# Block two's mixer in a new order, its bias outside the matmuls, and norms by logarithm and exponential

## The reference

```
h = rmsnorm(x);  x = x + 0.5 * swiglu(h)
p = rmsnorm(x) @ w_in          # 2048 columns: a, f (256 each), q, k, v (512 each)
y_pool = ((window means of a) - a) @ pool_w * pool_scale      # 4 groups, windows 2, 4, 8, 16
y_four = real(fft2(f)) @ fourier_w                            # over tokens and 64 features
s_j = q_j k_j^T / 8 - slope_h * |i - k|     for 4 heads h and the two halves j of a head
attn = softmax(s_0) - lambda * softmax(s_1)
y_attn = rmsnorm(attn @ v) * head_norm * (1 - lambda_init)
x = x + concat(y_pool, y_four, y_attn) @ w_out
h = rmsnorm(x);  x = x + 0.5 * swiglu(h)
```

## Time and profile before

| | |
|---|---|
| median of 3 runs | 2199.71 us (2198.16 to 2203.26) |
| profiled execution | 2203.84 us, span 2202.0 us |
| mean granted TensorE clock | 0.971 |
| TensorE busy | 2092.7 us, 95% |
| VectorE, ScalarE busy | 64%, 44% |
| mixer and output projection of block two, layer one | 1373 to 1488 us |
| the same, layer two | 1881.5 to 1996.5 us |
| HBM | 155 GB/s over the span |

### The profile page before, as it was taken

How to read it: one execution, slowest core, us unless ns; L and a number is a source line. 1 busy time by engine, 2 the same in 40 slices (tenths; PEclk the granted TensorE clock), 3 DMA queues, 4 the chain that set the end, 5 groups by cost and what they waited for, 6 DMA issues and landing times.

```text
span 2202.0 us, 42635 instructions
## 1 busy us (share of the span) xinstructions
PE 2092.7 (95%) x16256; PEld 2013.1 (91%) x16256; DVE 1411.6 (64%) x2402; ACT 970.9 (44%) x1402; POOL 181.6 (8%) x215
## 2 busy tenths in 40 slices
PE   8999888999999998889997999989998999989997
PEld 8999776999999987789997999979998999969997
DVE  6764646876577555567746775467754775566765
ACT  4434554443443345444434444344444443444443
POOL 0001200400130030030003000000000000000000
PEclk9999989999999998899998999999999999999999
DMA  6553322445354532235544564425554555414553
GB/s 238 179 196 136 115 77 77 153 168 198 129 180 165 196 122 77 84 111 189 197 185 145 176 214 163 139 73 172 178 209 137 172 198 184 153 58 168 177 207 136
DMA packets 44368, 343.12 MB, mean 156 GB/s; under 512 B 4848, under 2 KB 5872, under 8 KB 6256
## 3 DMA queue, kind: packets, MB, share of 16 engines
q1 hardware_dynamic: 43536, 335.63, 44.0%
q0 software_dynamic: 736, 6.17, 0.8%
HBM read 340.73 MB, written 1.05 MB: 155 GB/s over the span
## 4 chain that ended last, share of the span: by engine, by line
PE 86%; DVE 7%; ACT 2%; issue 2%; DVEq 1%; DMA 1%; POOL 0%; ACTq 0%; POOLq 0%; SPq 0%
PE ps L505 27%; PE ps L506 26%; PE ps L507 26%; DVE w_lo L1486 1%; ACT w_hi L1037 1%; DVE x_lo L1542 1%; DVE rstd L1549 0%; PE ps L764 0%; DVE scratch L1942 0%; PE ps L878 0%; DMA raw<-in_w_up 0%; PE ps L755 0%; ACT x_hi L1092 0%; PE ps L909 0%; DVEq L1516 0%
## 5 line engine op out<-in xcount | busy, mean ns | idle before, releaser
L505 PE MATMUL ps<-x_hi,w_lo 128*128 128x256 f32 (+3 forms) x3648 | 1071.2, 294 | 55.0 <-DVE x_lo L1542 24.4
L506 PE MATMUL ps<-x_lo,w_hi 128*128 128x256 f32 (+3 forms) x3648 | 1058.9, 290 | 0.0
L507 PE MATMUL ps<-x_hi,w_hi 128*128 128x256 f32 (+3 forms) x3648 | 1056.7, 290 | 0.0
L1486 DVE TENSOR_TENSOR w_lo<-raw,w_hi 128x1024 fp32r<-128x1024 f32 (+1 forms) x588 | 752.8, 1317 | 136.5 <-ACT w_hi L1037 130.9
L505 PEld LDWEIGHTS ps<-x_hi,w_lo 128*128 128x128 f32 x3648 | 710.5, 195 | 72.9 <-issue 32.8
L1037 ACT ACTIVATE w_hi<-raw 128x1024 fp32r<-128x1024 f32 (+1 forms) x588 | 633.4, 1120 | 325.2 <-PE ps L507 313.9
L506 PEld LDWEIGHTS ps<-x_lo,w_hi 128*128 128x128 f32 x3648 | 710.4, 195 | 0.6
L507 PEld LDWEIGHTS ps<-x_hi,w_hi 128*128 128x128 f32 x3648 | 710.1, 195 | 0.0
L507 PE MATMUL ps<-hid_hi,w_hi 128*128 128x256 f32 (+1 forms) x1408 | 400.3, 284 | 0.0
L505 PE MATMUL ps<-hid_hi,w_lo 128*128 128x256 f32 (+1 forms) x1408 | 398.0, 283 | 0.0
L506 PE MATMUL ps<-hid_lo,w_hi 128*128 128x256 f32 (+1 forms) x1408 | 396.9, 282 | 0.0
(11 more groups left out here) (235 smaller groups left out, 1258.4 us busy)
## 6 DMA issues: line engine op xcount, KB each, us to landing
raw<-in_w_up SPq DMA_DIRECT2D x178, 1024.0 KB, 4.9
raw<-in_w_down SPq DMA_DIRECT2D x64, 1408.0 KB, 6.0
raw<-in_w_in SPq DMA_DIRECT2D x36, 1024.0 KB, 4.9
raw<-in_w_out SPq DMA_DIRECT2D x16, 1024.0 KB, 5.0
cst<-in_consts POOLq DMA_DIRECT2D x1, 2176.0 KB, 9.6
cst<-in_consts POOLq DMA_DIRECT2D x1, 1537.5 KB, 6.7
prm<-in_prm POOLq DMA_DIRECT2D x2, 690.0 KB, 8.2
h<-in_hidden SPq DMA_DIRECT2D x1, 1088.0 KB, 7.1
```

Source lines behind the costliest of these rows:

```text
L505: mm(dst, w_lo[:, j, cols], xa, start=first, stop=False)
L506: mm(dst, w_hi[:, j, cols], xb, start=False, stop=False)
L507: return mm(dst, w_hi[:, j, cols], xa, start=False, stop=last)
L1486: v.tensor_tensor(w_lo[:, j, c], raw[:, j, c], w_hi[:, j, c].bitcast(F32), ALU.subtract)\
```

## The change

1. Input units of block two in a new order, set by tables `F0, A0`, `Q`, `K`, `V`: f, f, then q and k of head 0, 1, 2, 3, then v0..v3, then a, a. The host permutes the columns. Three PSUM banks in turn instead of four.
2. The steps of the Fourier part and of the heads stand between the units. TensorE's queue is: units 0 to 4, transposes of f, 5, scores 0, 6, sums over tokens, 7, scores 1, 8, sums over features, 9, transposes 0, scores 2, 10, Fourier product, 11, scores 3, v0, 12, transposes 1, output 0, v1, 13, output 1, v2, 14, transposes 2, v3, mean squares of heads 0 and 1, 15, output 2, transposes 3. Transposes of a, output 3, mean squares of heads 2 and 3 with the window means, and the pool product stand before chunks 1, 2, 3 and 5 of the first pair of the output projection. VectorE's and ScalarE's queues are rewritten to match, with the weight splits one unit at a time.
3. A score group has no bias matmul: its matmuls for the two row halves stand next to each other. VectorE adds the bias (fp32, in `cst`, over constants of block one) while it takes the maximum, four tensor_tensor_reduce a head into `prob2`; the exponentials read `prob2`.
4. The result chunks get their own place, `cat_hi2` and `cat_lo2`, in the memory of the feed-forward's hidden state. The projection takes them in the order 2, 3, 4, 5, 6, 7, 0, 1.
5. Every norm: logarithm, drain, exponential of minus a half of it, on ScalarE straight into `rstd`. The reciprocals go, on the head outputs too. The table set for both is loaded where the one for the root was, and at the end of each output projection.
6. In block two's output projection the first six x chunks of the next feed-forward are formed before the last two residuals, the last two behind their own.
7. Block two's layers are written out on TensorE, ScalarE and VectorE. SyncE and GpSimd keep their loops.
8. The second load of constants leaves out the old tables and a third one brings the bias, 1 MB; GpSimd's bf16 copy goes.

```diff
 def att_s(hh):
-    bank = S2_BANK[hh]
-    if hh == 3:
-        pe.wait_ge(exp2_done.sem, exp2_done.at(l, 2))
+    pe.wait_ge(proj2_ready.sem, proj2_ready.at(l, K[hh] + 1))
+    if hh > 0:
+        pe.wait_ge(nm2_ready.sem, nm2_ready.at(l, 4 * hh))
     for i in range(2):
         for j in range(2):
-            dst = ps[:, bank + j, 256 * i:256 * i + T2]
-            mm(dst, pj[head_rows(j), 4 + hh, P * i:P * i + P], pj[head_rows(j), 8 + hh, 0:T2],
-               start=True, stop=False)
-            last = mm(dst, slope_bf[:, hh, :], absd_bf[:, i, :], start=False, stop=True)
+            last = mm(ps[:, S2_BANK + j, 256 * i:256 * i + T2], pj[head_rows(j), Q[hh], P * i:P * i + P],
+                      pj[head_rows(j), K[hh], 0:T2], start=True, stop=True)
     last.then_inc(s2_ready.sem, 1)
...
 def block(i):
-    if i >= 4:
-        pe.wait_ge(proj2_ready.sem, proj2_ready.at(l, i - 3))
-    narrow_unit(turn0 + i // 4, (i // 2) % 2, i % 2, ps[:, i % 4, 0:T2], T2)
+    if i >= IN_BANKS:
+        pe.wait_ge(proj2_ready.sem, proj2_ready.at(l, i - IN_BANKS + 1))
+    narrow_unit(turn0 + i // 4, (i // 2) % 2, i % 2, ps[:, i % IN_BANKS, 0:T2], T2)
...
 def maxima(hh):                                   # VectorE
+    dve.drain()
     dve.wait_ge(s2_ready.sem, s2_ready.at(l, hh + 1))
-    s, bank = hh % 2, S2_BANK[hh]
-    v.reduce_max(amax[:, s, :], ps[:, bank:bank + 2, :].rearrange("p j (i k) -> p (j i) k", i=2), AX_X)
-    dve.drain()
-    v.tensor_scalar(nmax[:, s, :], amax[:, s, :], -ATT_SCALE, None, ALU.mult).then_inc(nm2_ready.sem, 1)
+    s = hh % 2
+    for j in range(2):
+        for i in range(2):
+            c = 2 * j + i
+            v.tensor_tensor_reduce(out=prob2[:, s, c, :], in0=ps[:, S2_BANK + j, 256 * i:256 * i + T2],
+                                   in1=alibi[:, hh, i, :], scale=-ATT_SCALE, scalar=3.0e38,
+                                   op0=ALU.add, op1=ALU.min, accum_out=nmax[:, s, c:c + 1])\
+                .then_inc(nm2_ready.sem, 1)
...
 def root(number, T, eps):                         # ScalarE
     act.wait_ge(var_ready, number + 1)
-    fn(std[:, 0, 0:T], ps[:, 7, 0:T], ACT.Sqrt, bias=con(eps, 1)).then_inc(std_ready, 1)
+    fn(std[:, 0, 0:T], ps[:, 7, 0:T], ACT.Ln, bias=con(eps, 1))
+    act.drain()
+    fn(rstd[:, 0:T], std[:, 0, 0:T], ACT.Exp, scale=-0.5).then_inc(std_ready, 1)
...
-def root(number, T, layer_norm=False):            # VectorE
+def root(number):
     dve.wait_ge(std_ready, number + 1)
-    last = v.reciprocal(rstd[:, 0:T], std[:, 0, 0:T])
-    if layer_norm:
-        last.then_inc(rstd_ready, 1)
-    dve.drain()
...
 def out_proj(turn0, resid, rms, norm, T, gain=None):   # ScalarE
     for p in range(OUTB // 2):
         if p > 0:
             split_next(turn0 + p // 2, p % 2, W_NARROW)
-        if p == OUTB // 2 - 1:
+        last = p == OUTB // 2 - 1
+        if rms and last:
+            for k in range(2 * p):
+                high(P2, gain, k, T, T2)
+        if last:
             second_pair(turn0 + OUTB // 4, 0)
-            load_sqrt()
+            load_log_exp()
         if rms:
             for u in range(2):
                 square(norm, resid, 2 * p + u, T)
-    if rms:
-        for k in range(KD):
-            high(P2, gain, k, T, T2)
+                if last:
+                    high(P2, gain, 2 * p + u, T, T2)
...
+return {1: a_transposes, 2: last_output, 3: last_means, 5: pool_out}     # TensorE, end of mixer2
...
-with pe.Fori(0, DEPTH) as l:                      # and the same on ScalarE and VectorE
+for l in range(DEPTH):
```

More of the change, by code:

```diff
@@ L516, in narrow_unit, with first_pair @@
                 last.then_inc(unit_used, 1)
-            def first_pair(turn, event, bank, T, xs=None, before=None):
+            def first_pair(turn, event, bank, T, xs=None, before={}, order=range(KD)):
                 xa, xb = xs or x_of(T)
                 pe.wait_ge(lo_done, turn * 4 + 2)
-                for k in range(KD):
-                    if before and k == before[0]:
-                        before[1]()
-                    pe.wait_ge(x_ready, event * KD + (k + 1))
+                for n, k in enumerate(order):
+                    if n in before:
+                        before[n]()
+                    pe.wait_ge(x_ready, event * KD + (n + 1))
                     for u in range(2):
@@ L1584, in out_proj @@
                         split_next(turn0 + p // 2, p % 2, W_NARROW)
+                    last = p == OUTB // 2 - 1
+                    if gain and last:
+                        for k in range(2 * p):
+                            low(number, P2, gain, k, T, T2)
                     for u in range(2):
-                        if p == OUTB // 2 - 1 and u == 1:
+                        if last and u == 1:
                             lo_unit(turn0 + OUTB // 4, 1, 0, W_NARROW)
@@ L1589, in out_proj @@
                         resid(alpha, 2 * p + u, bank + u, T)
-                if gain:
-                    for k in range(KD):
-                        low(number, P2, gain, k, T, T2)
+                        if gain and last:
+                            low(number, P2, gain, 2 * p + u, T, T2)
             def layer_norm(norm, gain, bias, next_turn, T):
@@ L1972, in mixer2 @@
+                scale(2)
+                weights(5)
+                lambda_sum()
+                scale(3)
+                weights(6)
+                scale(4)
+                weights(7)
+                scale(5)
+                weights(8)
+                maxima(0)
+                scale(6)
+                weights(9)
+                sine_sums()
+                scale(7)
+                weights(10)
+                difference(0)
+                scale(8)
+                weights(11)
                 maxima(1)
-                difference(0)
@@ L2021, in _ @@
             dve.drain().then_inc(prm_free, 1)
-            root(3 * DEPTH, T2)
-            with dve.Fori(0, DEPTH) as l:
+            root(3 * DEPTH)
+            for l in range(DEPTH):
                 t0, q = l * TURNS2 + BLOCK2_TURN, l * 2 + 2 * DEPTH
```

556 lines of the change are left out of this document (319 added, 237 removed).

## The result

Measured: 2138.81 us (median of 4 runs, 2129.02 to 2145.04) against 2198.93 for the kernel before on the same chip, ratio 0.9722 with a 95% interval of 0.9678 to 0.9767: 60 us faster. Forecast were 2151 and a range from 2138 to 2171, as a ratio 0.978 to the median of 2199.71. So the median lies 0.8 us inside the lower edge of the range, and by the ratio (0.9722 x 2198.93 = 2137.8) the time is 0.2 us outside it; the gain was 60 us where the sum had 49.2. The miss is a size, and it has to be found among the terms.

What follows compares the result with a forecast made beforehand. TensorE, busy 95% of the span, was taken as the bound: its work, waits and lower clock. Savings of 30.0 (terms 1 to 3), 11.9 and 7.3 (terms 4 and 5) make 49.2 us: 2199.71 becomes 2151, range 2138 to 2171.

Steps and rivals of the forecast that it cites:

- terms 4 and 5: Block two's layers written out instead of looped, 11.9 us; thirteen norms by logarithm and exponential without the reciprocal, 7.3 us.
- terms 1 to 3: Block two's mixer with output projection: scores 8.2, waits 3.4, clock 3.4; together 15.0 us a layer, 30.0 for both.
- term 2: TensorE waits behind the mixer's last input block: 8.8 us a layer go, 5.4 new ones in the projection, 3.4 saved.
- The list of places: Projection waits: head one's low part 0.3, head three's 1.1, pool chunk 1.6, first residual 0.8, last feed-forward chunk 1.6 us.
- term 3: Low TensorE clock in block two's mixer: 4.4 us a layer to regain, 1.0 left unpaid, 3.4 counted.
- term 1: Block two's scores without bias matmuls, row halves paired: a head from 3.36 to 1.3 us, 8.2 us saved a layer.
- rival 5: More than forecast: the waits in the projection and all of the low clock go too, 2139 us; chance 0.06.
- the signs that the prediction named: Mixer: busy about 12 us less, groups 1.3, no input wait over 0.5, projection waits 1 to 1.6; turn gap under 3.

Runs made afterwards that it cites:

- w1: The changed kernel without the table load at the end of block two's output projection; 2138.11 us, ratio 0.9717 to the kernel before.
- w4: The changed kernel with four 512-column copies, each with a drain, ahead of each head's exponentials on ScalarE; 2143.00 us, ratio 0.9733 to the kernel before.
- w2: The changed kernel with three 512-column copies, each with a drain, ahead of the logarithm of the second pair's norms on ScalarE; 2142.42 us, ratio 0.9727.
- w3: The changed kernel with all eight input chunks of the next feed-forward made behind all eight residuals; 2144.05 us, ratio 0.9738 to the kernel before.
- m1: The kernel before with layers written out and new norms, minus block two's bias matmuls (bias left out of the result), old order of work; 2170.83 us, ratio 0.9861.
- b1: The changed kernel without the projection's table load, with 64 unused bytes per partition ahead of split x and 64 more ahead of split hidden units; 2118.62 us, ratio 0.9633.

## Why the prediction was off

The direction holds, terms 4 and 5 were right within 1 us, and the savings come from where terms 1 to 3 placed them. The failed step is the size of terms 1 to 3, 15.0 us a layer, where the stretch gives 20.0 (117.0 - 97.0), and above all the waits that term 2 left in the projection:

- **Waits (term 2), the main error.** Forecast 8.8 - 5.4 = 3.4, measured 8.7 - 2.5 = 6.2. The list of places was right, the sizes were not: 0.3, 1.1, 1.6, 0.8 and 1.6 became 0, 0.56, 0.55, 0.16 and 1.20. For the second of them the trace says how it came to be too large (TensorE in the changed kernel, up to the row of 1426.60 above):

```profile
1422.23 1.02 PE L989 MATMUL ps<-scratch,cst 128*128 128x256 f32 x4
1423.18 1.95 PE L924 MATMUL ps<-cst,scratch 128*64 128x256 f32 x16
1425.07 0.39 PE L507 MATMUL ps<-hid_hi,w_lo 128*128 128x256 f32 x1
```

The chain from the mean squares to the chunk takes 4.37 us (1422.23 to 1426.60), even a little more than the 4.2 of the prediction. But TensorE works 3.81 of them: 0.95 for the mean squares, which the chain holds too, 1.89 for the window means and 0.97 for the chunk, where I had set only 1.9 and 0.72 against it (and 4.2 less these two is 1.6, not the 1.1 that I wrote). So the cover was too small there, not the chain too long. For the table load w1 shows that of the 1.28 us charged 0.46 was paid. For the pool chunk and the first residual the prediction gives no working, and why they came out at a third and a fifth stays open. w4 shows how well the chains ahead of all this are covered: of 11.2 us of delay 1.8 came through.
- **Clock (term 3).** Forecast 3.4, with 1.0 left unpaid; all 4.4 came back. Even the 4.1 us of waits in w2 left it at 1.00. That the waits are why it fell before is argued, not shown: for it speak the place (2.46 us and four more waits in some 24 us) and layer one of w3, against it that layer two of w3, with the longer wait, kept the full clock.
- **Scores (term 1).** Forecast 8.2; a group went from 3.19 to 1.06, 8.5 (it was 3.27 where a transpose followed, which can add 0.2 here and take it from the remainder below). I took both ends a little high: 3.36 counted a fourth bias in full, and two times 0.66 counted the changing over twice. That the whole of it appears on the path needs the new order: m1 gets 4 to 5.
- **Own place of the result chunks,** counted at nothing: 192 matmuls now stream from the faster tile, 0.0021 us each, 0.4. With small work that I did not price, the remainder is 0.9.

Together 2.8 + 1.0 + 0.3 + 0.9 = 5.0 a layer, 10.0 for both, which with 49.2 makes 59, against 60 measured. That is the figure of rival 5 (the waits in the projection and all of the low clock go too, 2139), to which I had given 0.06 and at which I had closed the range. Its mechanism came true only in part: all of the low clock went, but 2.5 of the 5.4 us of waits stayed, and the scores and the unpriced remainder made up for it. That the sum of these ended at its figure is luck. The chance was too small because I treated estimates that all leaned to the careful side as if their errors would cancel. Of the signs that the prediction named, most came: no wait between input blocks, no gap at the turn, the clock up in the projection. But the waits in the first pair are 0.16 to 0.56 us, not 1 to 1.6, a score group is 1.07 and not 1.3, and TensorE's busy time in the stretch fell by 13.8 us (108.29 to 94.53), not by about 12.

The prediction charged 1.28 us for the load at the end of the projection. That one loads the set that is in place, so w1 says nothing on a switch of set. A switch of set is the load of the earlier trace rows, and from it to the next instruction are 1.30 us. The 2.66 that the Trainium skill ("ScalarE: Activation LUTs", What ACT_TABLE_LOAD costs) gives for each switch to a different set isn't seen there.

## What to carry to other kernels

Each of the five waits that I found by walking the queues came out smaller than forecast. Against a chain that starts on TensorE count all that TensorE does in its time, the first step of the chain too, and give the case in which most of the waits vanish its own weight. Two savings on one stretch are not a sum: taking work off TensorE in front of an exposed chain turned half of it into waiting here (in one layer, into waiting and a lower clock in the other), and the order that covers the chain is what cashes it. Before comparing two profiles, compare a stage that the change does not touch.

## What I had not expected of the hardware

- The address of the streamed tile in SBUF sets the pace of fp32r matmuls: 0.1200 or 0.1179 us for 256 columns, 0.1292 or 0.1267 for 274, by a shift of 64 bytes. A shift by 128 bytes left the hidden units at 256 columns and x at 274 alone and brought x at 256 to 0.1187. With TensorE busy 96% of the time the two moves were worth some 18 us (b1 against the changed kernel, less the 0.9 of the table load; the intervals leave several us of doubt), more than the layers written out.
- fp32 matmuls in the two row halves run side by side even when two of one half come ahead of two of the other (1.07 us in both orders, 1.92 with one half).
- Unchanged code ran 17.6 us longer in one execution than in another by the granted clock alone (0.89 and 0.90 against 0.93 and 0.98 in the two mixers of block one).
- A wait of TensorE of 2.05 us was followed by a lower clock (0.77, then 0.89), one of 2.23 at the same place of the next layer by none.
